# A weight ring of seven or nine slots in the expert stage of a two-layer trunk kernel

## The reference, cut to what matters

```python
logits = (tok @ w_router).astype(jnp.float32) + b_router.astype(jnp.float32)
top_logit, top_idx = lax.top_k(logits, TOP_K)
top_w = jax.nn.softmax(top_logit, axis=-1)
gates = jnp.einsum("tk,tke->te", top_w, jax.nn.one_hot(top_idx, N_EXPERTS, dtype=jnp.float32))
for e in range(N_EXPERTS):
    y_e = _swiglu(tok, w_gate[e], w_up[e], w_down[e]).astype(jnp.float32)
    out = out + gates[:, e:e + 1] * y_e
```

## Time and profile before

| what | value |
|---|---|
| median of 3 runs | 1776.54 us |
| the profiled execution, time | 1776.94 us |
| its span in the profile | 1775.1 us |
| PE busy (matmul) | 1599.4 us, 90% |
| DVE, ScalarE (ACT), GpSimd (POOL) busy | 371.6, 217.9, 101.7 us |
| bytes moved on SP's queue | 481.51 MB |
| mean granted TensorE clock | 0.965 of full speed |
| share of the chain that ended last: PE, DMA, DVE | 72%, 11%, 6% |

### The profile page before, as it was taken

One profiled execution on the slowest core, in us unless ns is written; L12 is line 12 of the kernel. 1 busy time (PEld: TensorE's weight loads), 2 busy tenths in 40 slices (PEclk: granted clock), 3 DMA queues, 4 the chain that ended last, 5 costly groups with the idle time before them and its releaser, 6 DMA issues.

```text
span 1775.1 us, 24622 instructions
## 1 busy us (share of the span) xinstructions
PE 1599.4 (90%) x10871; PEld 912.8 (51%) x10872; DVE 371.6 (21%) x782; ACT 217.9 (12%) x416; POOL 101.7 (6%) x131
## 2 busy tenths in 40 slices
PE   7967899999999999997989999979979979887875
PEld 5633467777578866546343343345645653423322
DVE  1669320000055533403011001011011011110101
ACT  1411120000041133302000000000000000000001
POOL 5036200000000011100000000000000000000000
PEclk8988899999999999997999999999989989999999
DMA  9444576554384412332999977999969979999996
GB/s 330 150 147 167 189 279 250 220 218 150 113 311 143 143 48 75 116 142 96 382 403 409 362 290 267 404 408 408 403 250 347 388 266 397 403 409 404 409 408 248
DMA packets 167300, 485.81 MB, mean 274 GB/s; under 512 B 12928, under 2 KB 15872, under 8 KB 167168
## 3 DMA queue, kind: packets, MB, share of 16 engines
q1 hardware_dynamic: 157328, 481.51, 71.3%
q10 hardware_dynamic: 9840, 2.33, 0.7%
HBM read 482.78 MB, written 1.05 MB: 273 GB/s over the span
## 4 chain that ended last, share of the span: by engine, by line
PE 72%; DMA 11%; DVE 6%; issue 5%; SPq 2%; ACTq 1%; ACT 1%; POOL 0%; DVEq 0%
PE bank L1659 22%; PE bank L1209 20%; PE bank L1690 10%; DMA ring<-in_moe_w_down 8%; PE bank L1393 4%; PE bank L1584 3%; PE bank L1503 3%; DMA ring<-in_moe_w_up 3%; SPq L424 2%; PE bank L1636 2%; ACTq L530 1%; PE bank L1234 1%; DVE arena L921 1%; DVE arena L929 1%; PE bank L1542 1%
## 5 line engine op out<-in xcount | busy, mean ns | idle before, releaser
L1659 PE MATMUL bank<-ring,arena 128*32 128x256 f32 (+3 forms) x4864 | 510.0, 430 | 73.6 <-issue 46.6
L1659 PEld LDWEIGHTS bank<-ring,arena 128*32 128x32 f32 (+1 forms) x4864 | 230.1, 122 | 342.3 <-issue 267.7
L1209 PE MATMUL bank<-arena,ring 128*128 128x256 f32 x1280 | 287.0, 384 | 1.3 <-ACT arena L641 1.0
L1690 PE MATMUL bank<-ring,arena 128*32 128x256 f32 (+1 forms) x2128 | 253.2, 464 | 26.9 <-DMA ring<-in_moe_w_down 26.8
L1209 PEld LDWEIGHTS bank<-arena,ring 128*128 128x128 f32 x1280 | 243.9, 193 | 39.1 <-issue 4.5
L1690 PEld LDWEIGHTS bank<-ring,arena 128*32 128x32 f32 (+1 forms) x2128 | 103.1, 121 | 166.6 <-issue 119.6
L1134 DVE TENSOR_TENSOR arena<-arena,bank 128x512 f32<-128x512 f32 (+2 forms) x44 | 24.4, 576 | 607.8 <-PE bank L1659 607.8
L750 ACT ACTIVATE arena<-bank 128x512 f32<-128x512 f32 (+2 forms) x44 | 21.1, 508 | 696.7 <-PE bank L1671 576.4
L1393 PE MATMUL bank<-ring,arena 128*128 128x512 f32 x176 | 77.0, 595 | 0.3 <-PE bank L1209 0.3
L1234 PE MATMUL bank<-ring,cT 128*32 128x512 f32 x384 | 54.7, 695 | 8.9 <-ACT cT L583 8.3
L1503 PE MATMUL bank<-ring,arena 128*128 128x512 f32 x128 | 57.7, 593 | 0.3 <-PE bank L1209 0.3
(11 more groups left out here) (266 smaller groups left out, 1157.1 us busy)
## 6 DMA issues: line engine op xcount, KB each, us to landing
ring<-in_moe_w_gate SPq DMA_DIRECT2D x56, 2048.0 KB, 16.9
ring<-in_moe_w_up SPq DMA_DIRECT2D x56, 2048.0 KB, 16.8
ring<-in_moe_w_down SPq DMA_DIRECT2D x56, 2048.0 KB, 18.5
ring<-in_ada_w SPq DMA_DIRECT2D x24, 2048.0 KB, 9.1
ring<-in_m_w_in SPq DMA_DIRECT2D x12, 2048.0 KB, 9.1
ring<-in_ffn_w_gate SPq DMA_DIRECT2D x5, 2048.0 KB, 17.7
ring<-in_ffn_w_up SPq DMA_DIRECT2D x5, 2048.0 KB, 11.9
ring<-in_ffn_w_down SPq DMA_DIRECT2D x5, 2048.0 KB, 9.1
```

Source lines behind the costliest of these rows:

```text
L1209: ins = mm(out_, l, r, start=i == 0, stop=i == len(pairs) - 1, **kw)
L1659: ins = mm(ps[base + b // per][m * h:m * h + m, w * (b % per):w * (b % per) + w], hcur3[:, kc, m * b:m * b + m], sl[:, kc - half * rows, w ...
L1690: ins = mm(ps[4 + b // per][m * h:m * h + m, w * (b % per):w * (b % per) + w], actT[:, t % 2, b // per, n * (b % per) + i, m * q:m * q + m ...
```

## The change

The expert stage gets `MOE_RING` = 9 slots. Slots 7 and 8 are the arena's offsets 4096 to 12287. Expert tile n goes to slot n % 9. The first seven expert tiles wait as before for a layer-1 tile to be used, tiles 7 and 8 wait for `x_ready` = 6, and tile n from 9 on waits until expert tile n - 9 has been used. SP's loop over the experts is written out: 168 DMAs with constant addresses and constant counts. PE's matmuls are the same; a tile's slot and the count on its `ring_full` semaphore are now constants of tile n. The overflow path keeps seven slots and starts only when all tiles of the first pass have been used.

```diff
+MOE_RING = RING + 2
+FILLS0 = list(_fills) + [0] * (MOE_RING - RING)
+FILLS1 = [FILLS0[_s] + len(range(_s, NE * ITEM, MOE_RING)) for _s in range(MOE_RING)]
...
+            if s >= RING:
+                return area(4096 + (s - RING) * TILE, *shape)
...
-            def load_expert(e, k):
+            def load_expert(one, ready, place):
...
-                        sp.wait_ge(s["tile_used"], k * ITEM + (MOE0 + j - RING + 1))
+                        ready(j)
+                        at = place(j)
                         if what == "d":
-                            dst = slot(j % RING, 4, D)
-                            src = wd[bass.ds(e, 1), :, t * 8 + 4 * h:t * 8 + 4 * h + 4, :]
+                            dst = slot(at, 4, D)
+                            src = wd[one, :, t * 8 + 4 * h:t * 8 + 4 * h + 4, :]
...
-            with sp.Fori(0, NE) as e:
-                load_expert(e, e)
+            def first_pass_ready(n):
+
+                if n < RING:
+                    sp.wait_ge(s["tile_used"], MOE0 + n - RING + 1)
+                elif n < MOE_RING:
+                    sp.wait_ge(s["x_ready"], 6)
+                else:
+                    sp.wait_ge(s["tile_used"], MOE0 + n - MOE_RING + 1)
+
+            for e in range(NE):
+                load_expert(slice(e, e + 1), lambda j: first_pass_ready(e * ITEM + j),
+                            lambda j: (e * ITEM + j) % MOE_RING)
...
                 def expert_tile(what, t, h):
                     j = FIRST[what, t] + h
-                    pe.wait_ge(ring_full[j % RING], fill[j % RING] + 16 * (j // RING + 1))
-                    return j % RING
+                    if first_pass:
+                        n = k * ITEM + j
+                        at = n % MOE_RING
+                        pe.wait_ge(ring_full[at], 16 * (FILLS0[at] + n // MOE_RING + 1))
+                    else:
+                        at = j % RING
+                        pe.wait_ge(ring_full[at], k * 48 + 16 * (FILLS1[at] + j // RING + 1 - 3 * NE))
+                    return at
```

More of the change, by code:

```diff
@@ L92 @@
     _user[_s] = _i
-FILLS0 = list(_fills)
 ORDER = []
@@ L274, in hybrid_trunk @@
         s = {n: sem(n) for n in names}
-        ring_full = [sem(f"ring_full{i}") for i in range(RING)]
+        ring_full = [sem(f"ring_full{i}") for i in range(MOE_RING)]
         block = ctx.enter_context(nc.Block())
@@ L412, in load_expert @@
                         j = FIRST[what, t] + h
-                        sp.wait_ge(s["tile_used"], k * ITEM + (MOE0 + j - RING + 1))
+                        ready(j)
+                        at = place(j)
                         if what == "d":
-                            dst = slot(j % RING, 4, D)
-                            src = wd[bass.ds(e, 1), :, t * 8 + 4 * h:t * 8 + 4 * h + 4, :]
+                            dst = slot(at, 4, D)
+                            src = wd[one, :, t * 8 + 4 * h:t * 8 + 4 * h + 4, :]
                         elif m == 2:
-                            dst = slot(j % RING, 4, D)
-                            src = (wg if what == "g" else wu)[bass.ds(e, 1), :, 4 * h:4 * h + 4, t * D:(t + 1) * D]
-                        else:
-                            dst = slot(j % RING, KC, HALF)
-                            src = (wg if what == "g" else wu)[bass.ds(e, 1), :, :, t * D:t * D + HALF]
-                        sp.dma_start(dst, src.rearrange("e p k n -> p (e k) n")).then_inc(ring_full[j % RING], 16)
-            with sp.Fori(0, NE) as e:
-                load_expert(e, e)
+                            dst = slot(at, 4, D)
+                            src = (wg if what == "g" else wu)[one, :, 4 * h:4 * h + 4, t * D:(t + 1) * D]
+                        else:
+                            dst = slot(at, KC, HALF)
+                            src = (wg if what == "g" else wu)[one, :, :, t * D:t * D + HALF]
+                        sp.dma_start(dst, src.rearrange("e p k n -> p (e k) n")).then_inc(ring_full[at], 16)
+            def first_pass_ready(n):
[8 more added lines that the diff above has]
+                            lambda j: (e * ITEM + j) % MOE_RING)
             sp.wait_ge(s["cnt_ready"], 1)
@@ L432, in _ @@
                 with sp.If(over > 0):
+                    sp.wait_ge(s["tile_used"], MOE0 + NE * ITEM)
                     with sp.Fori(0, NE) as e:
@@ L435, in _ @@
                         with sp.If(n > 0):
-                            load_expert(e, sp.snap(items))
+                            k = sp.snap(items)
+                            load_expert(bass.ds(e, 1),
+                                        lambda j: sp.wait_ge(s["tile_used"], k * ITEM + (MOE0 + j - RING + 1)),
+                                        lambda j: j % RING)
                             sp.reg_add(items, items, 1)
@@ L1637, in scatter, with expert @@
                        y_sb[:, HALF * (i % 2):HALF * (i % 2) + HALF], start=True, stop=True).then_inc(s["scat_mm"], 1)
-            def expert(g, k, nb, m, after_gate, after_turns):
-                fill = [k * 48 + 16 * FILLS0[i] for i in range(RING)]
+            def expert(first_pass, g, k, nb, m, after_gate, after_turns):
                 parts, per = P // m, 64 // m
@@ L1715, in item @@
             def item(e, nb, m):
-                expert(e, e, nb, m, lambda: scatter(e - 1, gates_of[(e - 1) % 2]) if e else None,
+                expert(True, e, e, nb, m, lambda: scatter(e - 1, gates_of[(e - 1) % 2]) if e else None,
                        lambda: gather(e + 1, e + 1) if e + 1 < NE else None)
             def more(g, k):
-                expert(g, k, 2, 64, lambda: None, lambda: None)
+                expert(False, g, k, 2, 64, lambda: None, lambda: None)
                 scatter(k, gates_of[0])
```

## The result

The changed kernel takes 1754.86 us, the median of 4 runs (1751.05 to 1756.61); the kernel before takes 1777.76 us in the same comparison (4 runs, 1773.34 to 1780.08). The ratio is 0.987, with a 95% interval of 0.9851 to 0.989: 1.3% faster, by 1.1 to 1.5%. The profiled execution took 1756.61 us with a span of 1754.9 us.

What follows compares the result with a forecast made beforehand. Transfers and PE were taken to bound the expert stage in turns, by expert. Savings of 7.3 + 4.1 + 10.3 = 21.7 us gave a forecast of 1755 us, range 1749 to 1767.

Steps and rivals of the forecast that it cites:

- Tiles 7 and 8: Before expert 0: both loads start after x_ready at 801.4 us and land about 816 and 821 us.
- head start: Two tiles loaded in the idle stretch before expert 0, to remove its waits for weights, 7.3 us.
- Expert 0's waits: PE's five waits for weights in expert 0, 6.2 us, 7.3 with slower restarts, go entirely.
- Expert 2's waits: PE's three waits for weights in expert 2, 3.4 us, 4.1 with slower restarts, go entirely.
- Lead at the end: Transfer-bound experts 5 to 7: two more tiles already in place bring the last load 10.3 us earlier.
- Last load: End of expert stage: lands 21.7 us earlier, near 1736 us, with the tail after it unchanged.
- Waits in experts 6 and 7: PE's 40.9 us of waits for weights there shrink by some 6 us but do not vanish.
- The written-out loop: SP's expert loads: fewer small instructions per load, taken as 0, with 0 to 1 us of gain.
- Instruction gaps: PE's 41.9 us of gaps in the expert stage: change taken as 0, plus or minus 5 us.
- Rival 1: Only the lead at the end counts; something else replaces the waits in experts 0 and 2: 1766 us, chance 0.12.
- rival 2: The change does not deliver its slots in the expert stage, so nothing is gained: 1776 us, chance 0.06.
- rival 3: PE's instruction fetches at expert boundaries lose to the deeper load queue, making the kernel slower: up to 1827 us, chance 0.04.

Runs made afterwards that it cites:

- early half of the lead: Changed kernel, but loads wait on the tile nine places before only up to tile 62, seven places from tile 63 on: 1764.35 us, ratio 0.9946.
- The run with the lead only late: Changed kernel, but up to tile 62 loads wait on the tile seven places before, nine from tile 63 on: 1763.96 us, ratio 0.9935.
- light loads: Changed kernel moving only the first row block of each expert load, so experts compute with stale weights: 1688.36 us, ratio 0.9512.

## Why the prediction was right, point by point

- **Time.** 1755 us was forecast, 1754.86 us measured, in the range of 1749 to 1767. That the two meet within 0.2 us is luck: the gain, 21.7 us by the sum, is 22.9, 19.9 and 17.4 us in three comparisons, and from the use of tile 0 to the end of expert 7 the profiles of the full change are 18.5, 18.2 and 21.3 us faster than the kernel before. The mechanism is the one forecast; the sum is some 2 us high.
- **Tiles 7 and 8.** They were issued at 800.3 and 800.7 us and landed at 815.2 and 820.3 us (816 and 821 forecast). The head start is worth 8.2 us (7.3 forecast), by the run without it.
- **Expert 0's waits.** All 7.3 us were to go; 7.2 did.
- **Expert 2's waits.** 4.1 us forecast, 3.9 measured. The early half of the lead, both experts together, gave 10.7 us (11.4 forecast).
- **Lead at the end.** 10.3 us forecast; 10.2 in the profile and 5.2 with eight slots. The run with the lead only late gained 11.1 us, about 3 of which belong to expert 0; the 8 that are left are 2 less than the term, and experts 3 and 4 took 3.1 us back in that profile.
- **Last load.** Near 1736 us was forecast, 1736.7 measured. Here too two errors cancel: tile 0 was used 2.3 us earlier than in the kernel before, by chance, and experts 3 and 4 gave 2.8 us back.
- **Waits in experts 6 and 7.** They were to shrink by about 6 from 40.9 us; they are 33.9, 7 less.
- **The written-out loop.** Taken at 0; 1.0003 (0.9994 to 1.0012).
- **Instruction gaps.** Taken at 0 with 5 us either way. Over the stretch of the earlier trace rows they are 41.4, 43.4 and 43.3 us in the three profiles of the full change, against 41.9. The term was nevertheless a little too small: experts 3 and 4 take some 2 to 3 us longer with more than seven slots. The reason that I gave for 0 was too strong: that the gap at 1546 us is short with full engines, and that the two longest differ "by the version of code that was left, not by load". With a quarter of the traffic or less the two fall from 10.4 and 9.6 to 7.4 and 7.5 us, and the gaps of 2.6 us before experts 6 and 7 shrink to nothing and 0.3 us. Both act: load makes each longer, and the version sets where the long ones are.
- **Rivals.** Rival 1 (1766 us) is ruled out by the early lead's 10.7 us; rival 2 by the early issue and by all runs with more slots; rival 3, slower than before, by all timings of the change; what is left of it is the 2 to 3 us in experts 3 and 4.

## What to carry to other kernels

Where a stage alternates between bound by transfers and bound by compute, an extra buffer is worth one transfer time at each place where the lead runs dry before the next compute-bound part, but never more than the wait that stands there; only the last, unbroken transfer-bound stretch pays in full. So a gain per slot can be read from the waits: the first extra slot brought 13 us here, the second 7. A small price stood against it, 2 to 3 us where PE ran many short matmuls beside the longer burst of loads. And a transfer taken out of the last stretch does not pay if the matmuls behind the load before it become the bound: shortening the last one gained 0.7 us in the profile. Shortening one some tiles before the end left the last load as the bound, but its gain (3.5 us in the medians, about 1 us in the profile) is not settled.

## What the runs showed of the hardware that I had not expected

Weight traffic lengthens PE's instruction gaps in code with many short matmuls: with a quarter (or less) of the bytes moved, the gaps in the expert stage fell from 46.8 to 27.6 us, and expert 3, whose tiles are 96 matmul records each where expert 1's are 32, ran in 123.5 us instead of 136.6 (88 instead of 402 GB/s). Expert 1, with longer matmuls, took 156.1 us with either traffic. About 9 us more was PE being busy for longer: behind gaps of 2.5 to 3 us the granted clock was 0.50 to 0.86, and 1.00 in the same expert with light loads. A longer distance between a load and its tile (eight or nine instead of seven) cost 2 to 3 us in experts 3 and 4 in most profiles. The Trainium skill (Runtime: NRT & Kernel Launch, section Instruction fetch mechanics) says that crossing a block of instructions is mostly hidden and that a taken branch can stall the fetch. The trace agrees on the branches: the longest gaps, 10.4 and 9.6 us, lie where PE leaves experts 3 and 4 and jumps over versions that it does not run. In straight code it agrees for 81 us of expert 3 at 404 GB/s, and differs in that expert's shortest matmuls, where gaps of 0.4 to 2.5 us stand under full traffic and none with light loads, if these gaps are late fetches, as their places suggest.
